# A two-block transformer kernel on one core: the first norm reordered, two norms' sums moved inside the next unit, the last products added to the output by adding transfers

## The reference

```python
def rmsnorm(x, g):
    xf = x * lax.rsqrt(jnp.mean(x * x, axis=-1, keepdims=True) + EPS)
    return xf * g
# first block
xn = rmsnorm(h, norm1_gain);  proj = xn @ w_in          # attention, S5 layer, gates
h = h + (g_attn * attn_branch + g_ssm * ssm_branch) @ w_out
hn = rmsnorm(h, norm2_gain);  up = causal_dwconv(hn @ w_up, conv_w, conv_b)
h = h + (silu(gate) * val) @ w_down
# second block
m = hybrid_mixer(rms_norm(x, mix_norm_pre), ...)
x = x + rms_norm(m, mix_norm_post)
h = rms_norm(x, mlp_norm_pre)
x = x + rms_norm(squared_relu_mlp(h, w_ff_in, w_ff_out), mlp_norm_post)
```

## Time and profile before

| | us |
|---|---|
| median of 3 runs (lowest, highest) | 1477.43 (1476.66, 1480.17) |
| the profiled execution | 1480.89 |
| its span in the profile | 1479.1 |
| PE busy | 1414.4 (96%) |
| ACT busy | 829.7 (56%) |
| DVE busy | 658.1 (44%) |
| POOL busy (mostly issuing transfers) | 203.6 (14%) |
| moved by the DMA engines | 255.34 MB, mean 173 GB/s |

### The profile page before, as it was taken

How to read it: one execution, slowest core, us unless ns; L and a number is a source line. 1 busy time by engine, 2 the same in 40 slices (tenths; PEclk the granted TensorE clock), 3 DMA queues, 4 the chain that set the end, 5 groups by cost and what they waited for, 6 DMA issues and landing times.

```text
span 1479.1 us, 18389 instructions
## 1 busy us (share of the span) xinstructions
PE 1414.4 (96%) x6786; PEld 1120.0 (76%) x6786; DVE 658.1 (44%) x1153; ACT 829.7 (56%) x1159; POOL 203.6 (14%) x235
## 2 busy tenths in 40 slices
PE   3999999999899999999999999899999999999994
PEld 2887777677578878888888877677788888888883
DVE  4884345465533445555135154746555211212124
ACT  4644666676564566565455376555766655535431
POOL 0120110010011111111111111110111111111111
PEclk9999999999999999999999999999999999999997
DMA  8889876556359878888978997554576888887971
GB/s 256 192 177 185 206 163 145 130 125 150 93 116 245 194 172 198 188 190 192 217 167 196 216 227 172 128 140 113 130 173 141 191 198 188 197 204 176 205 151 57
DMA packets 80675, 255.34 MB, mean 173 GB/s; under 512 B 16592, under 2 KB 17744, under 8 KB 80464
## 3 DMA queue, kind: packets, MB, share of 16 engines
q0 software_dynamic: 32544, 118.50, 44.3%
q1 hardware_dynamic: 47616, 132.57, 29.4%
q10 hardware_dynamic: 432, 3.15, 0.6%
HBM read 128.09 MB, written 3.41 MB: 89 GB/s over the span
## 4 chain that ended last, share of the span: by engine, by line
PE 88%; DVE 4%; ACT 4%; DMA 2%; issue 1%; SPq 1%; POOLq 0%; POOL 0%; DVEq 0%; ACTq 0%
PE pg L500 26%; PE pg L502 25%; PE pg L501 25%; PE ps L637 2%; PE py L701 1%; DMA toep<-k_dram 1%; PE ps L799 1%; PE px L654 1%; PE ps L809 1%; DMA w_lo<-w_raw 1%; DMA w_raw<-weights 1%; PE px L532 1%; PE py L819 1%; ACT w_lo L901 0%; PE px L534 0%
## 5 line engine op out<-in xcount | busy, mean ns | idle before, releaser
L500 PE MATMUL pg<-x_hi,w_hi 128*128 128x512 f32 x1168 | 469.0, 402 | 10.7 <-DVE x_lo L1319 9.9
L502 PE MATMUL pg<-x_hi,w_lo 128*128 128x512 f32 x1168 | 457.8, 392 | 0.0
L501 PE MATMUL pg<-x_lo,w_hi 128*128 128x512 f32 x1168 | 457.6, 392 | 0.0
L468 POOL DMA_DIRECT2D w_lo<-w_raw x226 | 194.8, 862 | 1235.4 <-ACT w_lo L901 1209.1
L900 ACT ACTIVATE w_hi<-w_raw 128x1024 fp32r<-128x1024 f32 x226 | 237.6, 1051 | 123.8 <-PE pg L502 107.1
L500 PEld LDWEIGHTS pg<-x_hi,w_hi 128*128 128x128 f32 x1168 | 221.3, 189 | 64.2 <-issue 13.8
L501 PEld LDWEIGHTS pg<-x_lo,w_hi 128*128 128x128 f32 x1168 | 221.3, 189 | 47.5 <-issue 3.4
L502 PEld LDWEIGHTS pg<-x_hi,w_lo 128*128 128x128 f32 x1168 | 220.9, 189 | 47.2
L901 ACT ACTIVATE w_lo<-w_raw 128x1024 fp32r<-128x1024 f32 x226 | 236.4, 1046 | 0.0
L500 PE MATMUL pg<-act_hi,w_hi 128*128 128x512 f32 x432 | 168.0, 389 | 0.0
L501 PE MATMUL pg<-act_lo,w_hi 128*128 128x512 f32 x432 | 168.0, 389 | 0.0
(11 more groups left out here) (278 smaller groups left out, 1523.3 us busy)
## 6 DMA issues: line engine op xcount, KB each, us to landing
w_raw<-weights SPq DMA_DIRECT2D x226, 512.0 KB, 4.6
w_lo<-w_raw POOLq DMA_DIRECT2D x226, 512.0 KB, 5.7
kq_rot<-kq_raw SPq DMA_DIRECT2D x64, 64.0 KB, 2.4
hid<-x SPq DMA_DIRECT2D x4, 512.0 KB, 5.7
hid<-x ACTq DMA_DIRECT2D x1, 2048.0 KB, 11.0
out<-hid SPq DMA_DIRECT2D x8, 256.0 KB, 2.0
u_dram<-hid SPq DMA_DIRECT2D x4, 256.0 KB, 7.0
pairs<-u_dram SPq DMA_DIRECT2D x8, 128.0 KB, 7.4
```

The costliest lines, as they stand in the source:

```text
L468: pool.dma_start(w_lo[:, s], w_raw[:, s], accum_op=ALU.add).then_inc(lo_in[s], 16)
L500: pe.matmul(bank[:], wh, xh(k), start=n == 0, stop=False)
L501: pe.matmul(bank[:], wh, xl(k), start=False, stop=False)
L502: last = pe.matmul(bank[:], wl, xh(k), start=False, stop=n == len(ks) - 1)
```

## The change

1. **First norm.** Unit 0 is issued ahead of the constants. ACT squares all eight pieces into eight separate buffers (`sq_first`, inside `gates`), so no square waits for DVE. PE sums pieces 0, 1 and 2 itself, then the sum of pieces 3 to 6 that DVE makes with three adds, then piece 7. The ones are made by a DVE memset (`ones_first`). Unit 0 has no negated copy and no adding transfer: DVE subtracts `w_hi` from `w_raw` (semaphore `lo_first`). ACT converts unit 1 ahead of the inverse root, and unit 2 in the middle of the writing of `x_hi`. The counts of the slot's semaphore are lowered by one (`lows`).
2. **Second and third norm.** `statistic(2)` and `statistic(3)` are made ahead of the fourth `k` of the next unit. The table loads are put ahead of the eight pieces for norms 2, 3, 4 and 6.
3. **End.** DVE adds a piece's square ahead of its wait for the next bank. `hid` is stored to `out` by eight SP transfers between the loads of 16 units, from unit `("down2", 0, 0)` on. After the sixth norm DVE only multiplies; POOL issues, for each piece, an adding transfer `out` += `acc`.

```diff
+            weights_to(0)
             sp.dma_start(cst[:], consts).then_inc(c_landed, 16)
-            weights_to(0)
...
-            weights_range(sent, len(UNITS))
+            turn_out = UNIT[("down2", 0, 0)]
+            weights_range(sent, turn_out)
+            sp.wait_ge(res_done, KT)
             for k in range(KT):
-                sp.wait_ge(fin_pool if k % 2 else fin_done, k // 2 + 1)
-                sp.dma_start(out[:, k], hid[:, k]).then_inc(stored, 16)
-            sp.wait_ge(stored, 16 * KT)
+                sp.dma_start(out[:, k], hid[:, k]).then_inc(residual_out, 16)
+                for u in range(turn_out + 2 * k, turn_out + 2 * k + 2):
+                    next_weights(u)
+            weights_range(turn_out + 2 * KT, len(UNITS))
+            sp.wait_ge(residual_out, 16 * KT)
...
-            for m in range(1, KT, 2):
+            pool.wait_ge(residual_out, 16 * KT)
+            for m in range(KT):
                 pool.wait_ge(fin_mul, m + 1)
-                pool.tensor_tensor(hid[:, m], hid[:, m], acc[:, m], ALU.add).then_inc(fin_pool, 1)
+                pool.dma_start(out[:, m], acc[:, m], accum_op=ALU.add).then_inc(stored, 16)
+            pool.wait_ge(stored, 16 * KT)
...
+            def inside(n):
+                return lambda k: statistic(n) if k == 3 else None
...
-                if n > 1:
+                if n == 5:
                     ln_and_exp()
...
                     for m in range(KT):
+                        if (kind, c) == order[-1]:
+                            add_squares(6, m - 1)
                         evacuated(dve, ("down2", c - 1, m))
...
-                            add_squares(6, m - 1)
             root_ready(6)
             for m in range(KT):
                 put(stt(acc[:, m], acc[:, m], par("mlp_post", m), rstd[:]), fin_mul)
-                if m % 2 == 0:
-                    put(tt_(hid[:, m], hid[:, m], acc[:, m], ALU.add), fin_done)
```

More of the change, by code:

```diff
@@ L468, in lo @@
                 pool.dma_start(w_lo[:, s], w_raw[:, s], accum_op=ALU.add).then_inc(lo_in[s], 16)
-            for v in range(11):
+            for v in range(1, 11):
                 lo(v, v % RING)
@@ L534, in statistic @@
                 pe.matmul(px[:], ones, sqr[:, (KT - 1) % 2], start=False, stop=True).then_inc(px_full, 1)
+            pe.wait_ge(ones_made, 1)
+            for k in range(FIRST_ON_PE):
+                pe.wait_ge(sq_done, k + 1)
+                pe.matmul(px[:], ones_first, sq_first[:, k], start=k == 0, stop=False)
+            pe.wait_ge(sq_read, FIRST_ADDS)
+            pe.matmul(px[:], ones_first, sq_sum[1][:], start=False, stop=False)
+            pe.wait_ge(sq_done, KT)
+            pe.matmul(px[:], ones_first, sq_first[:, KT - 1], start=False, stop=True).then_inc(px_full, 1)
             pe.wait_ge(c_landed, 16)
-            statistic(1)
             x_use("lam")
@@ L769, in ffn @@
                                 first = a == 0 and i == begin and n == 0
-                                named((up, i), XH, XL, first_split=SPLIT[split_in] if first else None)
+                                named((up, i), XH, XL, first_split=SPLIT[split_in] if first else None,
+                                      ahead_of=inside(2) if first and stat_n == 3 else None)
                             if stat_n == 6 and i == KT + 3:
@@ L949, in _ @@
                 act.wait_ge(x_landed[k // 2], 16)
-                square(1, k, hid[:, k])
-                if k == 5:
-                    hi(0)
+                put(act.activation(sq_first[:, k], hid[:, k], ACT.Square), sq_done)
+            act.wait_ge(w_landed[0], 16)
+            put(act.activation(w_hi[:, 0], w_raw[:, 0], ACT.Copy), hi_done)
+            hi(1)
             act.wait_ge(c_landed, 16)
             inverse_root(1, rstd)
-            for u in range(1, RING - 1):
-                hi(u)
             for k in range(KT):
                 split_hi("norm1", k, x_hi[:, k], nrm[:, k % 2])
+                if k == 4:
+                    hi(2)
             act.wait_ge(p_landed, 16)
@@ L1285, in _ @@
                 else:
+                    if (kind, c) == order[-1]:
+                        ln_and_exp()
                     for m in range(KT):
@@ L1346, in scaled @@
                     split_lo(SPLIT[group] + k, x_lo[:, k], nrm[:, k % 2], x_hi[:, k])
-            for k in range(KT):
-                add_squares(1, k)
+            dve.memset(ones_first, 1.0).then_inc(ones_made, 1)
+            for k in range(FIRST_ON_PE + 1, KT - 1):
+                dve.wait_ge(sq_done, k + 1)
+                put(tt_(sq_sum[1][:], sq_first[:, k - 1] if k == FIRST_ON_PE + 1 else sq_sum[1][:], sq_first[:, k], ALU.add), sq_read)
+            dve.wait_ge(hi_done, 1)
+            dve.tensor_tensor(w_lo[:, 0], w_raw[:, 0], w_hi[:, 0].bitcast(F32), ALU.subtract).then_inc(lo_first, 1)
             dve.wait_ge(p_landed, 16)
```

38 lines of the change are left out of this document (27 added, 11 removed).

## The result

| | kernel before | changed kernel |
|---|---|---|
| median, us (lowest, highest; 4 runs each) | 1478.80 (1476.66, 1481.54) | 1468.63 (1466.23, 1469.07) |
| ratio of the times, 95% interval | | 0.9923 [0.9902, 0.9944] |
| the profiled execution, us | 1480.89 | 1468.54 |
| its span, us | 1479.1 | 1466.7 |

The change makes the kernel some 0.8% faster. The forecast was 1463.3, with a range of 1458.5 to 1470.0. The time is in the range and 5.3 us above the forecast. The two spans differ by 12.4 us, where -14.1 was forecast.

What follows compares the result with a forecast made beforehand. PE was taken as the bound (88% of the span), so gains come only where it waits. Terms -6.0 - 3.8 - 4.3 = -14.1 from a median of 1477.4 gave 1463.3 us, range 1458.5 to 1470.0.

Steps and rivals of the forecast that it cites:

- Start: First norm: the first `x_lo` comes at 18.7 instead of 25.0, with unit 1 late next; term -6.0 us.
- Joints: Second and third norm: sums inside the next unit save PE 1.9 us of waiting, twice; term -3.8 us.
- Last norm: End: PE makes the first sum right behind its last unit, so the sums end 2.65 us earlier.
- The residual's stores: Eight stores beside 16 units: the DMA share stays below 1 and PE busy; they cost nothing.
- Output: End, behind the norm: adding transfers replace sums and stores; -1.65 us, the rest of the end's -4.3.
- Eight in a line at 1.4: Output: eight adding transfers of 256 KB follow one another at 1.4 us each, ending the span at 1474.8.
- the median was 3.5 below that execution: Last step of the sum: the median lies 3.5 us below the profiled execution, so -14.1 is taken from 1477.4.
- (b): Rival, output: slow adding transfers of 2.0 to 2.4 us each, end +0.5 to +3.7, 1468.1 to 1471.3 us; chance 0.17.
- (a): Rival, output: adding transfers overlap so only POOL's issue counts, end -7.9, 1459.7 us; chance 0.17.
- (c): Rival, start: something with its own clock waits next, only 3.6 us of gain remain, 1465.7 us; chance 0.10.
- (d): Rival, second and third norm: the sums inside the units still wait, +3.8, 1467.1 us; chance 0.03.
- (e): Rival, output: adding transfers to memory from 3.2 us each make the whole slower, 1484.1 us at 4; chance 0.02.

Runs made afterwards that it cites:

- u_start: Changed kernel with the first norm, unit 0 and the order of the first transfers as before; 1473.62 us, ratio 0.9961.
- u_joint: Changed kernel with the sums of norms 2 and 3 made ahead of the next unit, as before; 1472.28 us, ratio 0.9946.
- mixed3: Changed kernel with three output pieces by adding transfers, five added on VectorE and stored by SyncE; 1463.92 us, ratio 0.9901.
- plain: Changed kernel with POOL's eight last transfers overwriting instead of adding, so the residual is missing from the output; 1464.85 us in one execution.
- pairs: Changed kernel with four adding transfers of 512 KB in place of eight of one piece; 1469.55 us in one execution.
- out_dve: Changed kernel without adding transfers, residual stores or POOL's sums: all eight output sums on VectorE, stores by SyncE; 1465.91 us, ratio 0.9912.

## Why the prediction was right, and where it was off

- **Start, forecast -6.0: about right.** The first `x_lo` came 6.9 earlier instead of 6.3. The step that was off is the sums' duration: five at the half-speed price of 1.9 were to end at 15.0, and they ended at 12.4, since the clock was up for the last two (1.02 for both passes). That gained nothing, because unit 1's copies on ACT, named as late next, held the inverse root until 15.0, 0.6 ahead of the forecast 15.6. Of the 6.9, PE's wait for `toep` takes some back: it is 1.0 instead of 0.3, and the matmuls on `toep` start 6.3 earlier (124.9 to 118.6). `u_start` gives 6 to 7. The error of 2.6 us in the sums did no harm because unit 1 and not the sums came last, as the prediction had said.
- **Joints, forecast -3.8: right.** Between the matmuls on `toep` and the one at 884.05 the difference grows from 6.3 to 10.6, by 4.3. Of this, 1.9 come at each of the two norms, as in `u_joint`: 3.8. Nearly all of the rest comes where the clock falls, near 385 and 425.
- **Last norm, forecast -2.65: right**, 2.64, with the clock still full in the second sum (1.13 for both passes), as was assumed.
- **The residual's stores, forecast nothing: right.** PE waits for nothing between 1060 and 1443, and the last matmul stands 10.66 earlier, as the one at 884.05 already does.
- **Output, forecast -1.65 behind the norm, was +0.90: the step that failed.** The term that was mis-sized is the price of an adding transfer to memory. The tail was to be 15.0 and is 17.5. "Eight in a line at 1.4" was nearly right for the steady part: 205 GB/s are 1.28 us for each 256 KB. But the first 741 KB took 5.8 us, 2.05 for each, and the first issue came 1.36 after the first product started, not 0.9. By the forecast's own formula (0.9 to the first issue, 2.1 fixed, 8t, 0.8 at the end) the tail of 17.5 means t = 1.7, where 1.4 was taken. The bound of 2.4 held, and what sets the price is that an adding transfer takes the engines 2.4 times as long as a plain one. The choice of 1.4 rested on a transfer that ran alone into SBUF, where the slow first part doesn't show; its window in the earlier trace rows (217 GB/s at a share of 1.12) did show that one adding transfer fills the engines.
- **From the sum to the median.** The terms give 1466.8 for the profiled execution, which took 1468.5, so they account for 1.7 of the 5.3: the output missed by 2.55, and start and joints together brought 0.86 more than forecast. The other 3.6 come from "the median was 3.5 below that execution". That median was of three runs. In the later groups the kernel before has medians of 1479.2 to 1480.8, so the three lay low, and the profiled execution, 1480.9, is near the middle of the ten runs beside the first group (1478.1 to 1481.9). The profiled execution of after is at its own median. That distance was chance and should not have been carried over.
- **Rivals.** The time fell where (b) had put it, 1468.1 to 1471.3, but by luck: (b) asked for 2.0 to 2.4 us for each transfer and an end 0.5 to 3.7 later than before, while the end came 1.7 earlier (2.64 from the norm, 0.90 lost) at 1.7 each, midway between the forecast and (b). The 3.6 of the median made up the rest. What (a) supposed holds for plain transfers only. Of (c) there was 0.7 us, the wait for `toep`. (d) and (e) did not occur.

## What to carry over

An adding transfer is cheap only where the DMA engines have time left: beside matmuls it is nearly hidden (PE waits 0.4 us for `w_lo` in the changed kernel, and 0.3 to 1.8 in the others), at the end of a kernel it takes the engines more than twice as long as a plain store, and everything behind it waits. At such an end compare it with the plain way, all sums on the idle vector engine and stores as they come, or with a few adding transfers only (a tail of 14.5 us, and 13.3 with three), and keep the general engine's sums off the vector engine's path. Take a sum of trace differences from one execution to the other and set the median apart, since the clock's falls near 385, 422 and 922 cost the other twelve traces 2.0 to 5.6 us more, over the same matmuls, than they cost that of `mixed3`.

## What was not expected of the hardware

- Adding transfers take the 16 DMA engines 13.6 us for 2.1 MB to memory and 12.6 into SBUF, plain ones 5.7. Rows of 4 KB instead of 2 KB give 12.0.
- Adding in memory starts slowly: 741 KB in the first 5.8 us, 205 GB/s after that. Into SBUF there is no such start: 160 to 195 GB/s throughout.
- POOL needs 0.89 us to issue an adding transfer in a line of eight and 0.54 for a plain one of the same size.
- Behind the last landing of POOL's transfers the span goes on for 3.6 us in `plain`, 3.2 in `pairs` and 1.4 in the changed kernel. Behind SP's stores in `out_dve` it is 0.4.
- Two DVE products of 0.75 us take 2.64 together beside one POOL sum of 1.25. Beside POOL's issues of transfers a product takes 0.78.
- The same wait of 2.8 us of PE was followed by the clock's fall to half in 6 of 13 traces, at 1.6 us in five of them and 2.8 in one, and one of 3.2 us in 12 of 13, at 0.9 to 2.3.
